# One step of a hybrid decoder trunk: sums of squares in two parts, dt as an fp32 product of its own, and the function table loaded early

## The reference

```python
h = rmsnorm(x, norm_mix_w)
a_b, a_c, a_x, z, xbc, dt_raw, g_a, g_b = split(h @ w_in)      # dt_raw: 32 columns, one for each head
br_a = (a_b * causal_conv3(a_c * a_x)) @ w_a_out
xs, bm, cm = split(silu(causal_conv4(xbc) + bias))
dt = softplus(dt_raw + ssd_dt_bias)
y = chunked_ssd_scan(xs, dt, -exp(ssd_a_log), bm, cm, state) + ssd_d * xs
gated = y * silu(z)                                            # 4 groups of 512 columns
gated = gated * rsqrt(mean(gated * gated, in each group) + eps) * ssd_norm_w
x = x + (sigmoid(g_a) * br_a + sigmoid(g_b) * (gated @ w_ssd_out)) @ w_o
x = x + peer(rmsnorm(x, norm_ffn_w))                           # 16384 experts, all multiplied, gated by 8 x top 16
return rmsnorm(x, norm_final_w), new states
```

## Time and profile before

| | us |
|---|---|
| three timed executions | 2409.12, 2412.52, 2415.19 |
| their median | 2412.52 |
| the profiled execution, its own time | 2407.87 |
| its span, first to last instruction | 2406.0 |
| mean granted clock | 0.995 |
| PE / PEld busy | 2380.0 / 2214.3 |
| DVE / ACT / POOL busy | 1607.6 / 837.2 / 1432.2 |

### The profile page before, as it was taken

The page is one execution under the profiler, slowest core; times in us unless marked ns, Lnnn a source line. Parts: engine busy times, 40 slices in busy tenths (PEclk is TensorE's granted clock), DMA queues, the critical chain, the costliest instruction groups (busy, mean ns, idle before and its releaser), DMA issues.

```text
span 2406.0 us, 38105 instructions
## 1 busy us (share of the span) xinstructions
PE 2380.0 (99%) x14550; PEld 2214.3 (92%) x14550; DVE 1607.6 (67%) x2611; ACT 837.2 (35%) x1279; POOL 1432.2 (60%) x787
## 2 busy tenths in 40 slices
PE   9999999999999999999999999999999999999998
PEld 8999999987899999999999999999989999999997
DVE  7865444455874353279897688888576766666664
ACT  4433223332231011233343355655433333333332
POOL 5554434332444555457676667777667777777762
PEclk9999999999999999999999999999999999999999
DMA  5224222237742233247776769999988888888872
GB/s 212 82 76 137 97 97 97 96 120 239 263 152 90 80 123 95 93 152 273 243 248 235 255 194 314 300 302 304 333 315 315 311 314 326 313 311 322 318 258 75
DMA packets 207742, 510.01 MB, mean 212 GB/s; under 512 B 15856, under 2 KB 104304, under 8 KB 205168
## 3 DMA queue, kind: packets, MB, share of 16 engines
q1 hardware_dynamic: 115552, 236.75, 30.9%
q10 hardware_dynamic: 55184, 137.07, 15.3%
q0 software_dynamic: 36864, 134.23, 15.0%
HBM read 424.55 MB, written 83.44 MB: 211 GB/s over the span
## 4 chain that ended last, share of the span: by engine, by line
PE 91%; DVE 5%; DMA 2%; ACT 1%; issue 1%; DVEq 0%; SPq 0%; ACTq 0%
PE ps L886 52%; PE ps L633 29%; PE ps L934 4%; DMA cxb<-parked_tiles 1%; DVE prev L1687 1%; PE ps L899 1%; PE ps L805 1%; PE ps L792 1%; PE ps L800 1%; PE ps L809 1%; PE ps L825 1%; PE ps L658 0%; DMA gbuf<-gate_scratch 0%; PE ps L778 0%; DVE hu_lo L1516 0%
## 5 line engine op out<-in xcount | busy, mean ns | idle before, releaser
L582 POOL TENSOR_SCALAR w_hi<-raw 128x1024 fp32r<-128x1024 f32 x129 | 138.9, 1076 | 520.8 <-issue 390.2
L609 POOL TENSOR_TENSOR w_lo<-raw,w_hi 128x1024 fp32r<-128x1024 f32 x128 | 324.3, 2534 | 188.3 <-PE ps L886 187.5
L609 POOL TENSOR_TENSOR w_lo<-raw,e_hi 128x1024 fp32r<-128x1024 f32 x128 | 324.5, 2535 | 177.8 <-PE ps L886 170.2
L886 PE MATMUL ps<-p_hi,w_lo 128*128 128x448 f32 x1024 | 376.2, 367 | 0.0
L886 PE MATMUL ps<-g_hi,w_lo 128*128 128x448 f32 x1024 | 375.6, 367 | 0.0
L584 POOL TENSOR_TENSOR w_lo<-raw,w_hi 128x1024 fp32r<-128x1024 f32 x129 | 318.5, 2469 | 10.8
L633 PE MATMUL ps<-h_hi,w_hi 128*128 128x296 f32 (+1 forms) x1216 | 274.3, 307 | 1.6 <-ACT ma L1201 1.6
L633 PE MATMUL ps<-h_lo,w_hi 128*128 128x296 f32 (+1 forms) x1216 | 262.5, 297 | 0.0
L633 PE MATMUL ps<-h_hi,w_lo 128*128 128x296 f32 (+1 forms) x1216 | 262.1, 297 | 0.0
L1295 ACT ACTIVATE e_hi<-raw 128x1024 fp32r<-128x1024 f32 x128 | 135.9, 1061 | 261.5 <-DMA raw<-units 120.4
L633 PEld LDWEIGHTS ps<-h_hi,w_hi 128*128 128x128 f32 x1216 | 196.1, 188 | 26.5 <-issue 23.8
(11 more groups left out here) (332 smaller groups left out, 5430.8 us busy)
## 6 DMA issues: line engine op xcount, KB each, us to landing
raw<-units SPq DMA_DIRECT2D x385, 512.0 KB
gate_scratch<-gt SPq DMA_DIRECT2D x56, 512.0 KB
activation_scratch<-ge ACTq DMA_DIRECT2D x120, 224.0 KB
abuf<-activation_scratch ACTq DMA_DIRECT2D x30, 896.0 KB, 5.8
gbuf<-gate_scratch ACTq DMA_DIRECT2D x30, 896.0 KB
prev<-ssm_in ACTq DMA_DIRECT2D x8, 1024.0 KB, 6.7
ssm_s<-prev ACTq DMA_DIRECT2D x8, 1024.0 KB, 4.5
parked_tiles<-stage ACTq DMA_DIRECT2D x24, 296.0 KB, 2.1
```

The lines of the kernel that those rows point to most:

```text
L582: pool.tensor_scalar(w_hi[:, s, :], raw[:, r, :], 1.0, 1.0, ALU.mult, ALU.mult).then_inc(s_whi, 1)
L609: pool.tensor_tensor(w_lo[:, n % 2, :], raw[:, n % RAW, :], e_hi[m % HS_].bitcast(F32), ALU.subtract)\
L886: last = mm(accp[par], w[:, k * P:(k + 1) * P], x_[:, k, t0:t0 + ND], start=k == 0 and i == 0, stop=k == KT - 1 and i == 2)
```

## The change

- dt has no unit any more, so there is one unit less, and the four units of the mixer are units 0 to 3. dt's 32 weight columns come as an array of their own (`w_dt`, 128 KB) by a DMA ahead of the first unit, and DVE multiplies them by the norm weight in front of `hu_lo`. TensorE multiplies them with the loaded x in fp32: 8 k tiles x 2 halves, k tile k on column tile k % 4, so that four partial sums of 32 rows stand side by side. The k tiles 0 to 3 come before k tile 0 of unit 0 and the others before its k tile 4. ACT copies the four partial sums out, and two fp32 matmuls with stacked identities (`stack4`) add them, after k tile 3 of unit 1. `spread_out(0)` moves from behind the first k tile of the third unit to behind the second unit.
- ACT makes `stack4` and the `fold` tables (10 copies) before it waits for x, so that its first function table is loaded then.
- The sums of the last square (`group_last`, `last_squares`) come two k tiles after those of the added squares (one k tile in the middle of the kernel; directly behind them, as before, at the end). `spread_out(1)` moves from k tile 6 to k tile 7.

```diff
-N_DT, N_XBC, N_A, N_Z, N_GB, N_GA, N_AO, N_SO, N_WO, N_WQ = 1, CT, 3 * KT, XT, KT, KT, KT, 2 * KT, KT, 2 * KT
+N_XBC, N_A, N_Z, N_GB, N_GA, N_AO, N_SO, N_WO, N_WQ = CT, 3 * KT, XT, KT, KT, KT, 2 * KT, KT, 2 * KT
 N_PARK = N_A + N_Z + N_GB
 N_PRE = 4
-N_RAW = 5
+N_RAW = 4
 WARM = 20
 KEEP = 14
 Q_RAW = 4
 XR = -(-T // P)
-U_DT = 0
-U_PRE = U_DT + N_DT
+U_PRE = 0
 U_XBC = U_PRE + N_PRE
 U_PARK = U_XBC + N_XBC
 U_GA = U_PARK + N_PARK - N_PRE
...
+            sp_.dma_start(wdt[:], w_dt).then_inc(s_wdt, 16)
             sp_.dma_start(raw[:, 0, :], units[0]).then_inc(ld[0], 16)
...
             def added_squares(r):
 
-                tiles = (sqa, squares_of(XT + KT - 1))
                 pe.wait_ge(s_sqa, (KT - 2) * (r - GROUPS))
-                turn_sums(*tiles, True, False)
+                turn_sums(sqa, False)
+
+            def last_squares(r):
+
                 pe.wait_ge(s_sq, XT + KT * (r - GROUPS))
-                turn_sums(*tiles, False, True)
-
-            def group_sums(g):
+                turn_sums(squares_of(XT + KT - 1), True)
+
+            def group_added(g):
 
                 pe.wait_ge(s_sga, 2 * g + 2)
-                turn_sums(sqg[0], sqg[1], True, False)
+                turn_sums(sqg[0], False)
+
+            def group_last(g):
+
                 pe.wait_ge(s_sq, 4 * g + 4)
-                turn_sums(sqg[0], sqg[1], False, True)
+                turn_sums(sqg[1], True)
 
...
-            as_ready(U_DT, U_DT, hu, s_u, 0)
-            tile(U_DT + 1, U_DT + 1, *hu)
-            part(U_DT + 2, 0, 1, hu)
+
+            def dt_products(ks):
+
+                for h in range(2):
+                    for k in ks:
+                        c = k % 4 * HEADS
+                        last = mm(dtp[c:c + HEADS, h], wdt[:, k, :], x[:, k, h * HF:(h + 1) * HF],
+                                  start=k < 4, stop=k >= 4)
+                return last
+
+            pe.wait_ge(s_dtw, 1)
+            for q_ in range(2):
+                for i in range(2):
+                    pe.wait_ge(s_x[2 * q_ + i], 16)
+                last = dt_products(range(4 * q_, 4 * q_ + 4))
+                if q_:
+                    last.then_inc(s_dtp, 1)
+                for k in range(4 * q_, 4 * q_ + 4):
+                    pe.wait_ge(s_u, k + 1)
+                    part(U_PRE, k, k + 1, hu)
+            part(U_PRE + 1, 0, 4, hu)
+            pe.wait_ge(s_dtc, 1)
+            for h in range(2):
+                last = mm(dtp[0:HEADS, h], stack4[:], dt_parts[:, h * HF:(h + 1) * HF], start=True, stop=True)
+            last.then_inc(s_dtp, 1)
+            part(U_PRE + 1, 4, KT, hu)
             spread_out(0)
-            part(U_DT + 2, 1, KT, hu)
-            for n in range(U_DT + 3, N_RAW):
+            for n in range(U_PRE + 2, N_RAW):
                 tile(n, n, *hu)
             as_ready(N_RAW, N_RAW, (h_hi, h_lo), s_h, 0)
 
             first_tile(U_AO, U_AO, v, s_v)
-            group_sums(0)
-            part(U_AO + 1, 0, 6, v)
+            group_added(0)
+            part(U_AO + 1, 0, 2, v)
+            group_last(0)
+            part(U_AO + 1, 2, 7, v)
             spread_out(1)
-            part(U_AO + 1, 6, KT, v)
+            part(U_AO + 1, 7, KT, v)
             for g in range(1, GROUPS):
                 n = U_AO + 2 * g
                 part(n, 0, KT, v)
                 pe.wait_ge(s_nf, 4 * g)
-                group_sums(g)
-                part(n + 1, 0, KT, v)
+                group_added(g)
+                part(n + 1, 0, 2, v)
+                group_last(g)
+                part(n + 1, 2, KT, v)
                 spread_out(1 + g)
             first_tile(U_SO, U_SO, (n_hi, n_lo), s_n)
             for j in range(1, KT):
@@ -859,6 +898,8 @@
             for k in range(KT):
                 if k == 6:
                     added_squares(1 + GROUPS)
+                elif k == 7:
+                    last_squares(1 + GROUPS)
                 pe.wait_ge(s_u, KT + k + 1)
                 part(U_WQ, k, k + 1, gu, L)
             part(U_WQ + 1, 0, 4, gu, L + 1)
...
+            act.wait_ge(s_c, 1)
+            for i in range(4):
+                a = slice(i * HEADS, (i + 1) * HEADS)
+                act.activation(stack4[a, :], ident[a, a], ACT.Copy)
+                if i < 2:
+                    b = slice(i * TS, (i + 1) * TS)
+                    act.activation(fold[a, :], ident[a, a], ACT.Copy)
+                    act.activation(fold2[b, :], ident[b, b], ACT.Copy)
+                else:
+                    act.activation(fold[a, 0:HEADS - HPG // 2], ident[a, i * HEADS + HPG // 2:(i + 1) * HEADS],
+                                   ACT.Copy)
...
-            act.wait_ge(s_unit, 1)
-            act.activation(halves(sp[0][:]), acc[0][0:HEADS], ACT.Copy).then_inc(s_accf[0], 1)
             deviation(0)
-            act.wait_ge(s_c, 1)
-            for i in range(2):
-                a, b = slice(i * HEADS, (i + 1) * HEADS), slice(i * TS, (i + 1) * TS)
-                act.activation(fold[a, :], ident[a, a], ACT.Copy)
-                c0 = (i + 2) * HEADS
-                act.activation(fold[c0:c0 + HEADS, 0:HEADS - HPG // 2],
-                               ident[c0:c0 + HEADS, c0 + HPG // 2:c0 + HEADS], ACT.Copy)
-                act.activation(fold2[b, :], ident[b, b], ACT.Copy)
+            act.wait_ge(s_dtp, 1)
+            act.activation(halves(dt_parts[:]), dtp, ACT.Copy).then_inc(s_dtc, 1)
+            act.wait_ge(s_dtp, 2)
+            act.activation(halves(sp[0][:]), dtp[0:HEADS], ACT.Copy).then_inc(s_dtc, 1)
...
+            dve.wait_ge(s_wdt, 16)
+            dve.wait_ge(s_col, 16)
+            tt_(wdt[:], wdt[:], col[:, COLS["mix"]:COLS["mix"] + KT].unsqueeze(2).to_broadcast([P, KT, HEADS]),
+                ALU.mult).then_inc(s_dtw, 1)
...
-            dve.wait_ge(s_accf[0], 1)
+            dve.wait_ge(s_dtc, 2)
```

More of the change, by code:

```diff
@@ L137, in gathers_after, with trunk @@
     return [j + UG for j, (_, c) in enumerate(ROWS) if max(c + 2, UT[0] + 2) == m and j + UG < len(ROWS)]
-def trunk(nc, xT, x_rows, units, keys, cols, heads, hist_a, hist_s, ssm_in, rows_u, rows_v,
+def trunk(nc, xT, x_rows, w_dt, units, keys, cols, heads, hist_a, hist_s, ssm_in, rows_u, rows_v,
           yT, new_a, new_s, ssm_p, ssm_s):
@@ L324, in trunk @@
         ssp = ps[:, 4:6, 0:HF]
+        dtp = ps[:, 4:6, 0:HF]
         inv = ps[:, 6:8, 0:HF]
@@ L357, in trunk @@
         s_dts = sem("dt_scaled")
+        s_wdt = sem("dt_weights_loaded")
+        s_dtw = sem("dt_weights_scaled")
+        s_dtp = sem("dt_products")
+        s_dtc = sem("dt_copied")
         s_tap = sem("first_tap_done")
@@ L652, in tile, with turn_sums @@
                     unit(n + u, L, mov_hi, mov_lo, u * KT, u == 0, u == units_ - 1)
-            def turn_sums(added, last_squares, first, last_one):
+            def turn_sums(squares, last_one):
                 nq = TK // NT
                 for i in range(NT):
-                    last = mm(turned[0:nq, i:i + 1], (last_squares if last_one else added)[:, i * nq:(i + 1) * nq],
-                              ones[:, 0:1], start=first and i == 0, stop=last_one and i == NT - 1)
+                    last = mm(turned[0:nq, i:i + 1], squares[:, i * nq:(i + 1) * nq],
+                              ones[:, 0:1], start=not last_one and i == 0, stop=last_one and i == NT - 1)
                 if last_one:
@@ L2063, in inputs_of @@
     aB, aC, aX, z, xbc, dt, ga, gb = (wi[:, o[i]:o[i + 1]] for i in range(8))
-    dt_p = np.zeros((D, P), wi.dtype)
-    dt_p[:, :HEADS] = dt
+    w_dt = np.ascontiguousarray(dt.reshape(KT, P, HEADS).transpose(1, 0, 2))
     units = np.empty((UNITS, P, D), wi.dtype)
-    units[U_DT:U_PRE] = tiles(dt_p)
     units[U_XBC:U_PARK] = tiles(xbc)
@@ L2096, in inputs_of @@
     x_rows = np.ascontiguousarray(x_rows.reshape(XR, P, D).transpose(1, 0, 2))
-    return dict(xT=xT, x_rows=x_rows, units=units, keys=keys, cols=cols, heads=heads, hist_a=hist(state_conv_a, KT),
+    return dict(xT=xT, x_rows=x_rows, w_dt=w_dt, units=units, keys=keys, cols=cols, heads=heads, hist_a=hist(state_conv_a, KT),
                 hist_s=hist(state_conv_ssd, CT), ssm_in=ssm,
```

6 lines of the change are left out of this document (5 added, 1 removed).

## The result

| | before | changed |
|---|---|---|
| median of 9 timed executions each, us | 2412.52 | 2419.87 |
| their range | 2408.47 to 2415.19 | 2418.01 to 2425.03 |
| profiled execution, its span | 2407.87, 2406.0 | 2421.96, 2420.0 |
| mean granted clock | 0.995 | 0.994 |
| PE / DVE / POOL busy | 2380.0 / 1607.6 / 1432.2 | 2381.3 / 1599.6 / 1429.3 |

The account below looks back on a forecast made before the run. On average only TensorE's work was taken to count (busy 2380 of 2406 us), except where other chains make it wait. dt 1.2 + sums 4.6 - middle block 0.1 = 5.7 us: median 2412.52 to 2406.8, range 2401.5 to 2413.5.

Parts of the forecast that it names:

- TensorE's price of dt: At the start, 16 fp32 products run four column tiles at a time: 2.0 us, plus 1.0 us for adding partial sums.
- rival 4: At the start, column tiles don't run together, inverse root 7.2 us late: 2413.1 us, or 2417.6 without the sums' gain; chance 0.15.
- rival 1: TensorE's account holds, VectorE's chain doesn't gate 87 us or the groups: 10.5 us gained, 2402.0 us; chance 0.20.
- The unit's gain is idle time: Ahead of 87 us, TensorE comes 4.7 us sooner but can't pass before `dqT`, so all that gain is idle.
- The start of VectorE's chain: At the start, the inverse root reaches VectorE at 28.3 us against 27.42, 0.9 us later.
- 0 to 2.1 us that POOL stops less: Ahead of 87 us, POOL's splits stop VectorE's chain less, saving 0 to 2.1 us; the upper end was taken.
- the lower bound of - 1.0: Worst case for dt's gain, forecast at 1.2 us with bounds - 1.0 and + 2.5.
- No fall behind parted sums: With 1.6 us of full matmuls between the halves, no clock falls expected; four falls had cost 6.0 us.
- The period of 16.6 us: VectorE's chain sets 16.6 us between groups' sums; three periods of 16.15, 16.6, 16.6 total 49.4 for 52.6, 3.2 us gained.
- The lower bound for the sums (- 1.5): Worst case for the sums' 4.6 us gain: splits still stop VectorE, 18.4 us a period, only the last group gains.
- Middle block: In the middle block the last square is long there, so parting the sums gains nothing and loses 0.1 us.
- (2): The clock still falls, partly between the groups' halves; groups worth 0.0 to - 1.0, dt's gain stays: 2411.5 us; chance 0.15.

Follow-up runs that it names:

- early_light: Kernel before with one of three products left out of units 6 and 7, ahead of TensorE's wait at 87 us; 2410.13 us, ratio 0.9996.
- late_light: Kernel before with one of three products left out of units 12 and 13, behind TensorE's wait at 87 us; 2408.05 us, ratio 0.9989.
- dt_only: Changed kernel with the sums in one go again, as before; 2413.97 us, ratio 1.0011 to the kernel before.
- dt_spread_sooner: dt_only with the first spread of the inverse root two k tiles sooner; 2410.36 us, ratio 0.9999 to the kernel before.
- parted_refilled: Kernel before with the groups' sums parted, middle block in one go, VectorE's gating and branch A outputs reordered; 2406.51 us, ratio 0.9984.
- after_refilled: Changed kernel with VectorE's order of parted_refilled; 2413.00 us, ratio 1.0004 to the kernel before.
- all_mended: after_refilled with the middle block's sums in one go and the first spread two k tiles sooner; 2405.45 us, ratio 0.9978 to the kernel before.
- sums_light_gates: Kernel before with the sums parted and the gating multiplies of groups 1 to 3 cut to one column each; 2414.11 us, ratio 1.0013.
- after_both_first: Changed kernel with VectorE's next gating and even branch A output ahead of the wait for a group's sums; 2417.46 us, ratio 1.0021 to the kernel before.
- sums_split_waits: sums_only with GpSimd's splits of three units held until VectorE has written a branch A output; 2411.82 us, ratio 1.0016 to the kernel before.
- sums_only: Kernel before with the sums parted and nothing else; 2416.52 us, ratio 1.0019.

## Why the prediction was wrong, step by step

- **TensorE's price of dt: right.** 2.20 us for the first 16 records and 1.20 for the second: four tiles together, no rival 4. (What TensorE saves ahead of 87 us stands as 4.7 us in one place of the prediction and as 4.9 in rival 1; the forecast uses neither.)
- **The unit's gain is idle time: right**, shown by `early_light` and `late_light`.
- **The start of VectorE's chain: mis-sized.** I had 28.3; it was 29.25. Unit 0 ended at 20.2 for 19.4. The second x tile came at 9.44 and not at 8.4, but that isn't the reason: in `dt_only` it came at 8.60, unit 0 ended at 20.0 and the chain began at 29.09. The terms behind it were each a bit short there: 2.1, 1.1 and 1.1 us for dt's two blocks and the addition (I had 2.0, 1.0 and 1.0), 3.4 us for each four k tiles (I had 3.2 to 3.3). The 0.9 us became 1.8.
- **"0 to 2.1 us that POOL stops less": mis-sized**, taken at the wrong end. It was 0.1 us (57.65 and 57.51). dt cost 1.5 to 1.7 us where I had a gain of 1.2, and the lower bound of - 1.0 didn't hold it either. In `dt_spread_sooner` the point moved the other way by 3.0 us, so the splits' part is larger than the 2.1 us that I allowed.
- **No fall behind parted sums: right for the groups.** With two k tiles between, none followed a pair of halves that TensorE ran without waiting; `parted_refilled`, `after_refilled` and `all_mended` have none in four groups. It doesn't hold for the middle block, with one k tile between: in `sums_light_gates` (halves at 904.61 and 906.48) and `after_both_first` (905.66 and 907.53) a fall of 3.4 us began at 907.8 and 909.1 with TensorE busy throughout, in the other five kernels with that block parted none did. The Trainium skill (TensorE: Matmul & The Clock Gate, The two states you'll see) names idleness as the cause; here the falls behind the waits for `ma` (from 702.5 us on) agree with that, those of before with TensorE busy don't.
- **The period of 16.6 us: the step that failed.** From the first half of one group's sums to the next it was 16.4, 24.7 and 19.0 us, where I had 16.15, 16.6 and 16.6. It failed in three places. I let TensorE wait only for the fourth normed tile (L1795), and passed over the instruction behind it on VectorE, the output that frees the accumulator of the unit just being begun. In the kernel before it ends at 698.20 and TensorE needs it at 698.67, a margin of 0.5 us; with the sums parted it needs it 1.0 us sooner behind their start:

```profile
697.45 0.75 DVE L1773 TENSOR_TENSOR ma<-ma,ps 128x576 f32<-128x576 f32 x1
```

```profile
698.67 0.51 PE L633 MATMUL ps<-v_hi,w_hi 128*128 128x288 f32 x2
```

  I wrote that the second split falls on instructions that read PSUM; it fell on the two last `n_lo` and cost 2.8 us. And I put no price on a clock that falls behind the new wait: 13.7 us at the low clock, 11.0 of them with TensorE at work. By the prediction's own price (1.5 us for 3.41) that is an estimated 4.8 us, most of the 6.0 that the four falls had cost before. The lower bound for the sums (- 1.5) had the splits in it, but in VectorE's period and not as idleness of TensorE.
- **Behind the spreads**, I had the root 1.7 us later but not the even output behind it, for which TensorE waited 2.08 us.
- **Middle block: mis-sized**, 1.4 us for 0.1: the root's last instruction, of both operands in SBUF, was pushed onto a split:

```profile
916.76 2.83 DVE L1530 TENSOR_TENSOR spread<-ident,root 72x576 f32<-72x576 f32 x1
919.65 1.24 PE L696 MATMUL ps<-spread,ones 72*128 72x288 f32 x4 [1.19 <-DVE spread L1530]
```

- **The rivals**: (2) comes nearest, in that the low clock came back and the groups gained nothing, but its mechanism is another: it came back behind waits. The one on the slower side was on column tiles; that of the group norms was missing.

## What to carry to other kernels

Where a step on the path is parted, list each instruction that stands behind it on every engine until the next time round, with who needs it and by how much it is early; the one with the smallest margin decides, not the longest. Where two engines stop each other, a shift of a microsecond is not worth a microsecond: it is worth whatever meeting it makes or avoids. A slow stretch can be what gives another engine its time; ask who used it before taking it away. And what shortens TensorE's way pulls in the work that its units release, here the splits, onto the engine that was just in time.

## What the runs showed of the hardware

- An idle TensorE is paid twice. In the second group seven kernels had a wait of 3.7 to 3.8 us and three one of 2.7 us, and in all ten the clock was low for 3.4 to 13.7 us from within the wait on (3.4 in `after_both_first`, 13.7 in the changed kernel); with a wait of 0.97 us there (`sums_split_waits`) it did not. Of six waits of 1.9 to 2.1 us in the groups, three were followed by a fall.
- The scan of the samples has falls of 6.8 us too, none, one or two of them between 530 and 620 us with the same program there; in `sums_only` TensorE was busy for 5.3 of the 6 us ahead of either, and so it was in `parted_refilled` (527 to 533 us), where none came. By the price of a fall each costs an estimated 3.0 us. They can account for part of the spread of single times (2405.44 to 2422.95 us for the kernel before in one series), so edits of a few microseconds show in the timeline before they show in a median.
- A scan over 32 partitions and 592 columns took 1.38 or 3.46 us, by whether a split ran beside it: a stop of 2.1 us for one instruction, however short. A copy of 3 columns (L1614) took 2.25 us from 61.61 on in the kernel before, where it took 0.17 at 78.55; it ended at 63.86 and the split's second instruction at 63.82. Instructions with an operand in PSUM weren't stopped (`h_lo<-ps,h_hi` at 34.66: 0.78 us beside the split of 34.45 to 36.86). The Trainium skill (GPSIMD Engine Reference, 2. Architecture) says that GpSimd's way to SBUF is shared with VectorE; the rows agree, and show the one instruction waiting for the other's end.
